# Eleven expert tiles in place of thirteen in a mixture-of-experts layer, with six blocks given out by the counts

## The reference, cut to what matters

```python
g_idx = top_1(softmax(hf @ w_rg + b_rg))          # group, 4 of them
e_idx = top_2(softmax(le[g_idx]))                 # 2 experts in the group
combine = weights of the 2 chosen experts, 0 for the other 14
a = einsum('bsd,edf->bsef', h, w_gate)
u = einsum('bsd,edf->bsef', h, w_up)
hid = silu(a) * u * combine
x = x + einsum('bsef,efd->bsd', hid, w_down)
```

## Time and profile before

| | |
|---|---|
| median of 3 runs | 499.16 us (497.79 to 499.41) |
| profiled execution | 500.98 us |
| its span, first to last instruction | 499.1 us |
| mean granted TensorE clock | 0.976 |
| expert part, first gate_up to the end | 323.1 to 499.1 us |
| PE busy | 466.0 us, 93% of the span |

### The profile page before, as it was taken

One profiled execution on the slowest core, in us unless ns is written; L12 is line 12 of the kernel. 1 busy time (PEld: TensorE's weight loads), 2 busy tenths in 40 slices (PEclk: granted clock), 3 DMA queues, 4 the chain that ended last, 5 costly groups with the idle time before them and its releaser, 6 DMA issues.

```text
span 499.1 us, 7640 instructions
## 1 busy us (share of the span) xinstructions
PE 466.0 (93%) x2826; PEld 227.5 (46%) x2826; DVE 214.7 (43%) x660; ACT 147.6 (30%) x340; POOL 152.8 (31%) x163
## 2 busy tenths in 40 slices
PE   5999999999999999999999999897999999998982
PEld 2545544445555565555556556633333333343320
DVE  2133644434764545355556757645122222231310
ACT  1321512326555555444342543400001011000000
POOL 1150788774499910000000211210351111111121
PEclk9999999999999999999999999778999999999997
DMA  8999960007000000193010459888499999999531
GB/s 308 396 412 367 404 266 1 1 0 270 5 1 1 1 2 0 49 412 131 0 44 2 145 195 378 309 314 325 153 358 384 391 374 403 388 375 400 183 57 26
DMA packets 28873, 102.66 MB, mean 206 GB/s; under 512 B 3744, under 2 KB 5280, under 8 KB 28448
## 3 DMA queue, kind: packets, MB, share of 16 engines
q1 hardware_dynamic: 22640, 88.25, 45.8%
q0 software_dynamic: 4176, 8.42, 7.0%
q10 hardware_dynamic: 2016, 5.46, 2.9%
HBM read 79.50 MB, written 29.44 MB: 218 GB/s over the span
## 4 chain that ended last, share of the span: by engine, by line
PE 77%; DMA 13%; DVE 4%; issue 2%; ACT 2%; POOL 1%; POOLq 0%; SPq 0%; DVEq 0%; ACTq 0%
PE bank L1344 21%; PE bank L1683 14%; PE bank L1514 10%; PE bank L1328 6%; PE bank L1707 6%; DMA arena<-in_w_gu 6%; PE bank L1416 5%; PE bank L1433 5%; PE bank L1379 3%; DMA arena<-slot_rows 3%; DMA slot_rows<-arena,small 3%; PE bank L1664 2%; PE bank L1457 2%; DMA arena<-in_w_in_lat 1%; DVE arena L1001 1%
## 5 line engine op out<-in xcount | busy, mean ns | idle before, releaser
L1344 PE MATMUL bank<-arena 128*128 128x512 f32 (+1 forms) x256 | 111.1, 584 | 5.7 <-DMA arena<-in_w_in_lat 5.7
L1683 PE MATMUL bank<-arena 128*32 128x512 f32 x832 | 96.3, 614 | 1.8 <-DMA arena<-in_w_gu 1.8
L1344 PEld LDWEIGHTS bank<-arena 128*128 128x128 f32 x256 | 48.2, 195 | 53.7 <-issue 53.2
L637 POOL DMA_INDIRECT out<-arena x13 | 20.2, 1550 | 134.3 <-DVE arena L1274 101.3
L1328 PEld LDWEIGHTS bank<-arena 128*128 128x128 f32 (+1 forms) x356 | 42.8, 140 | 35.7 <-issue 33.9
L1514 PE MATMUL bank<-arena 128*128 128x512 f32 x112 | 54.1, 605 | 0.6 <-issue 0.6
L1683 PEld LDWEIGHTS bank<-arena 128*32 128x32 f32 x832 | 26.8, 113 | 59.9 <-issue 57.5
L1328 PE MATMUL bank<-arena 128*128 128x128 f32 (+1 forms) x356 | 51.4, 277 | 2.7 <-ACT arena L711 1.9
L1707 PE MATMUL bank<-arena 128*32 128x512 f32 x416 | 47.1, 593 | 1.0 <-DVE arena L1267 1.0
L1001 DVE COPY arena<-bank 128x512 f32<-128x512 f32 (+2 forms) x64 | 35.7, 580 | 20.5 <-PE bank L1328 20.5
L873 ACT ACTIVATE arena<-bank 128x256 f32<-128x256 f32 x13 | 5.0, 383 | 129.7 <-PE bank L1683 129.7
(11 more groups left out here) (176 smaller groups left out, 502.4 us busy)
## 6 DMA issues: line engine op xcount, KB each, us to landing
arena<-in_w_gu SPq DMA_DIRECT2D x17, 2048.0 KB, 22.1
arena<-in_w_dn SPq DMA_DIRECT2D x17, 1024.0 KB, 22.7
slot_rows<-arena SPq DMA_DIRECT2D x1, 11822.0 KB, 48.3
arena<-slot_rows ACTq DMA_DIRECT2D x10, 514.0 KB, 7.3
arena<-in_w_out SPq DMA_DIRECT2D x2, 2048.0 KB, 8.1
arena<-in_x_turned SPq DMA_DIRECT2D x4, 512.0 KB, 8.1
arena<-in_x SPq DMA_DIRECT2D x4, 512.0 KB, 13.3
arena<-in_w_in_k SPq DMA_DIRECT2D x1, 2048.0 KB, 14.8
```

The lines of the kernel that those rows point to most:

```text
L1344: last = nc.tensor.matmul(product_bank(i)[:, 0:width], hT[:, t, k, :], w[:, k, :], start=(k == 0), stop=(k == KD - 1))
L1683: last = nc.tensor.matmul(GU[g % 2][BLK * b:BLK * (b + 1), :], xT[g % 2][:, k, BLK * b:BLK * (b + 1)], w_gu[n % RING][:, k, :], start=(k = ...
```

## The change

ITEMS becomes 11, and no extra tile runs unless the counts ask for it (up to 15 can, under conditions). The tiles are laid out by a table, in which FREE is a block whose place is found at run time:

```diff
-CAP, BLK = 96, 32
-ITEMS = E * CAP // P
+LAYOUT = [[0, 1, 2, 3], [0, 0, 1, 1], [2, 2, 3, 3], [4, 4, 5, 5], [FREE, 6, 6, 7], [FREE, 7, 8, 8], [FREE, 9, 9, 10],
+          [FREE, 10, 11, 11], [FREE, 12, 12, 13], [FREE, 13, 13, 14], [14, 14, 15, 15]]
+ITEMS = len(LAYOUT)
+LAST_USE = [1, 1, 2, 2, 4, 4, 5, 5, 6, 9, 8, 9, 9, 9, 9, 10]
+BUFFER = [0, 1, 2, 3, 4, 5, 0, 1, 2, 3, 4, 5, 0, 1, 2, 4]
+EXTRA = 15
-        LAST = ITEMS
+        LAST = ITEMS - 1
```

```diff
-            for g in range(LAST):
-                for n in range(RING, E + 1):
-                    if last_item(n - RING) == g - 1:
-                        sp.wait_ge(s_dn, 2 * g)
-                        load_dn(n, expert(n))
...
+            for g in range(ITEMS):
+                for n in range(RING, E):
+                    if LAST_USE[held_before(n)] == g:
+                        sp.wait_ge(s_gu, g + 1)
+                        load_gu(n, n)
+                for n in range(RING, E):
+                    if LAST_USE[held_before(n)] == g - 1:
+                        sp.wait_ge(s_dn, 2 * g)
+                        load_dn(n, n)
```

A token can have its two rows in one tile now, one in the free block and one in an own block. So a tile with a free block is added in two DMAs, 32 rows and then all 128 with the first 32 masked, and each add waits for the one before:

```diff
+            def add_rows(g, at, n):
+                nc.gpsimd.indirect_dma_start(
+                    out=out_rows, out_offset=bass.IndirectOffsetOnAxis(ap=at[0:n], axis=0),
+                    in_=y_sb[g % 2][0:n], in_offset=None,
+                    bounds_check=SEQ - 1, oob_is_err=False, compute_op=ALU.add).then_inc(s_add[g % 2], 16)
...
+                if loads_of(g)[0] == FREE:
+                    add_rows(g, tag_row[:, g, 0:1], BLK)
+                    pool.wait_ge(s_add[g % 2], added_before(g) + 16)
+                    add_rows(g, own_row[:, g - FREE_0, 0:1], P)
+                else:
+                    add_rows(g, tag_row[:, g, 0:1], P)
...
-            for g in range(ITEMS):
-                if g >= 2:
-                    added(g - 2)
+            for g in range(LAST):
+                if g > 0:
+                    added(g - 1)
                 add(g)
                 if g < 2:
                     overflow(2 * g)
                     overflow(2 * g + 1)
```

Rows for free blocks come with the overflow sends. So ACT loads no rows of tile 4 or a later one before all those sends have landed, and PE turns no tile in step 2 and two in step 3:

```diff
+            silu(0)
+            act.wait_ge(s_disp[1], 16 * TOP * 2)
+            load_x(3)
+            left_y(0)
+            silu(1)
+            silu(2)
+            left_y(1)
+            act.wait_ge(s_over, 16 * TOP * T)
+            for g in (4, 5, 6):
+                load_x(g)
+            for g in range(3, LAST + 1):
...
+        def turned_in(g):
+
+            return {2: (), 3: (4, 5)}.get(g, (g + 2,) if g + 2 <= LAST else ())
```

The matmuls of a free block take their weights from an address in a register, read twice a tile:

```diff
+                        if n == FREE:
+                            w = arena[:, bass.ds(free_at[g][0] + k * 2 * F, 2 * F)]
...
+            def free_places(g):
+
+                if g == FREE_0:
+                    pe.wait_ge(s_free, 1)
+                i = g - FREE_0
+                free_at[g] = [pe.value_load(v[0:1, i:i + 1], min_val=0, max_val=int(max(kbs) * KB))
+                              for v, kbs in ((gu_at, GU_KB), (dn_at, DN_KB))]
```

More of the change, by code:

```diff
@@ L58 @@
 K_FLOOR = K_LOW + E
-NK = K_FLOOR + E
+K_CAP = K_FLOOR + E
+K_FROM = K_CAP + E
+K_END = K_FROM + E
+K_MOST = K_END + E
+K_GU = K_MOST + E
+K_DN = K_GU + E
+K_LEAST = K_DN + E
+K_GONE = K_LEAST + FREES
+K_OWN = K_GONE + FREES
+NK = K_OWN + 1
+GU_KB = (16, 48, 120, 32, 64, 0)
+DN_KB = (80, 171, 195, 179, 187, 136)
 TILES = ITEMS + EXTRA
@@ L331, in loads_of, with buffer_of, nth_load, held_before @@
         def loads_of(g):
[L333 to L338, removed]
+            return LAYOUT[g] if g < ITEMS else [E + g - ITEMS] * 4
+        def buffer_of(n):
+            return BUFFER[n] if n < E else n % RING
+        def nth_load(n):
+            return sum(buffer_of(m) == buffer_of(n) for m in range(n + 1))
+        def held_before(n):
+            return max(m for m in range(n) if BUFFER[m] == BUFFER[n])
+        def own_loads(g):
+            return sorted(set(loads_of(g)) - {FREE})
+        def adds_of(g):
+            return 16 * (2 if loads_of(g)[0] == FREE else 1)
         def added_before(g):
-            return 16 * (g // 2)
+            return sum(adds_of(i) for i in range(g % 2, g, 2))
         def passes(eng, extra):
@@ L349, in passes @@
             with ExitStack() as more:
-                for i in range(1, EXTRA):
+                for i in range(EXTRA):
                     more.enter_context(eng.If(tiles > i))
@@ L1213, in extras_out @@
[L1213 to L1220, removed]
+                link(nc.vector.tensor_tensor(beyond, counts, table(K_CAP), ALU.subtract))
@@ new lines, in extras_out @@
+                link(nc.vector.tensor_scalar(wanted, beyond, 1.0, None, ALU.is_gt))
+                for bound in range(BLK, max(FREE_MOST) * BLK, BLK):
+                    link(nc.vector.scalar_tensor_tensor(wanted, beyond, bound + 1.0, wanted, ALU.is_gt, ALU.add))
+                link(nc.vector.tensor_tensor(wanted, wanted, table(K_MOST), ALU.min))
+                link(nc.vector.tensor_copy(sum_a, wanted))
+                running(sum_a, sum_b, ALU.add)
+                link(nc.vector.tensor_tensor(sum_a, sum_a, wanted, ALU.subtract))
@@ L1221, in extras_out @@
+                link(nc.vector.scalar_tensor_tensor(x_rows, f_blocks, -float(BLK), beyond, ALU.mult, ALU.add))
+                link(nc.vector.tensor_scalar(x_tmp, x_rows, 1.0, None, ALU.is_gt))
+                for bound in range(P, SEQ, P):
+                    link(nc.vector.scalar_tensor_tensor(x_tmp, x_rows, bound + 1.0, x_tmp, ALU.is_gt, ALU.add))
+                link(nc.vector.tensor_copy(x_start, x_tmp))
+                running(x_start, x_end, ALU.add)
                 link(nc.vector.tensor_copy(x_end, x_start))
@@ L1299, in _ @@
                 tile_tags(g)
+            places_out()
+            extra_places_out()
             for g in range(1, LAST + 1):
@@ L1780, with block_row, table @@
     p = np.arange(P, dtype=f32)
-    mine = (P * p[:ITEMS] + p[:, None]) // CAP
-    mine[:, 0] = p // BLK
-    for g in (1, 2):
-        mine[:, g] = 2 * (g - 1) + p // (2 * BLK)
+    mine = np.repeat(np.array(LAYOUT, f32).T, BLK, axis=0)
+    def block_row(n, i):
+        at = [P * g + BLK * b for g, row in enumerate(LAYOUT) for b, m in enumerate(row) if m == n]
+        return at[i]
+    def table(v):
+        return np.tile(np.array(v, f32), (P, 1))
+    least = [min(n for n in range(E) if FIRST_USE[n] <= g <= LAST_USE[n]) for g in FREE_TILES]
     konst = np.concatenate([
         np.triu(np.ones((P, P), f32), 1), np.ones((P, P), f32), np.tile(p[:E], (P, 1)),
-        np.tile(np.where(p[:E] < EARLY, P - BLK + 2 * BLK * p[:E], CAP * p[:E]), (P, 1)), np.tile(p[:EXTRA], (P, 1)), np.tile(p[:E] % G, (P, 1)), p[:, None] + P * p[:T] - FAR,
-        np.full((P, 1), FAR), mine, np.tile(np.where(p[:E] < EARLY, BLK - P - BLK * p[:E], 0), (P, 1)),
-        np.tile(np.where(p[:E] < EARLY, BLK, 0), (P, 1))], axis=1).astype(f32)
+        table([block_row(n, 1) - BLK for n in range(E)]), np.tile(p[:EXTRA], (P, 1)), np.tile(p[:E] % G, (P, 1)),
+        p[:, None] + P * p[:T] - FAR, np.full((P, 1), FAR), mine,
+        table([block_row(n, 0) - block_row(n, 1) + BLK for n in range(E)]),
+        np.tile(np.where(p[:E] < EARLY, BLK, 0), (P, 1)),
+        table([BLK * b - 0.5 for b in BLOCKS]), table(FREE_FROM), table([min(d, FREE_TILES[-1]) + 1 for d in LAST_USE]),
+        table(FREE_MOST), table([GU_KB[BUFFER[n]] * 256 for n in range(E)]),
+        table([DN_KB[BUFFER[n]] * 256 for n in range(E)]), table(least), table([float(g == GONE_AT) for g in FREE_TILES]),
+        np.where(p < BLK, 2 * FAR, FAR)[:, None]], axis=1).astype(f32)
     def by_expert(v, blocks):
```

182 lines of the change are left out of this document (118 added, 64 removed).

## The result

| | before | after |
|---|---|---|
| median | 498.48 us (4 runs, 497.73 to 499.41) | 509.8 us (4 runs, 509.05 to 510.76) |
| ratio to before | | 1.0224 (95%: 1.0191 to 1.0257) |
| span of the profiled execution | 499.1 us | 509.0 us |
| mean granted TensorE clock | 0.976 | 0.949 |
| matmuls in the expert part that gate and up take (L1683, L1819) | 832 | 704 |

The account below looks back on a forecast made before the run. PE was taken to bound the kernel, with weights close behind. 499.1 - 25.1 (tiles) + 18.2 (stall and clock) + 20.9 (chain of adds) = 513.1 us, forecast as 513 us, range 492 to 526.

Parts of the forecast that it names:

- The tiles: PE, expert part: two tiles of 11.68 us and a 1.76 us weight wait go, 25.1 us less.
- DVE: Counting before hidden(0): 29 more operations make it 1.6 us late, covered by other waits; cost 0, without cover 3.3 us.
- Registers: PE reading weight addresses into registers: hidden behind queued matmuls, cost 0, upper bound 12 us over six tiles.
- The stall: PE before tile 4 idles 14 us for overflow rows; with the lower clock, 18.2 us added.
- The pairs: Tiles 4 to 9: a 32-row then a 128-row add in series, 18.6 us loaded, 11.3 quiet; chain adds 20.9 us.
- Weights: Weight loads for PE: every gate_up finds its weights, cost 0; the stream alone would give about 485 us.
- the end: After the pairs end at 505.6 us, tile 10's add lands 6.0 us later and 1.5 us end the span: 513.1.
- (1): Adds at their quiet price all along: end at 496.9 us, or 492.2 if PE binds; chance 0.18.
- (2): Sends land before 378 or rows come at once, adds hidden: 474 us by PE, 485 by weights; chance 0.08.
- (3): Dearer adds, the 32-row add at a full one's price, pairs of 20.4 and 13.8 us: 525 us; chance 0.07.
- (4): Not eleven tiles, an extra tile runs through another routing: at least 15 us more, 528 us; chance 0.05.

Follow-up runs that it names:

- early sends: Changed kernel with all eight overflow sends right after the add of tile 0, not half behind the add of tile 1: 496.06 us, 0.9974 of before.
- a quarter of the weights: Changed kernel whose gate, up and down weight loads for places 10 to 15 move a quarter of their bytes: 495.51 us.
- both costs and the order of loads removed: Changed kernel with all overflow sends after tile 0's add, no 32-row adds, and down loads ahead of gate and up loads from step 5: 485.31 us.
- both edits: Changed kernel with all eight overflow sends right after the add of tile 0 and without the 32-row adds: 489.9 us.

## Why the prediction was right, point by point

**The tiles.** Two steps of PE went, and its cadence stayed 11.68 us. Right. PE's busy time fell by 19.3 us and not by 23.4, for some of the work ran at the lower clock level.

**DVE.** hidden(0) ran at 337.43 instead of 336.05, 1.4 us late (forecast 1.6). A thing that wasn't forecast came with it: PE idled 3.61 us and down(0) ran at the lower clock level, 6.39 us instead of 3.64 (granted clock 0.56 in 339.1 to 345.4). So gate_up(1) started 0.9 us later than before (347.57 against 346.66), although its rows were there. It ended at 354.6 us in both kernels all the same, because it took 7.07 us at the full clock and 8.01 before, part of it at the lower level. That the cost is 0 is partly luck.

**Registers.** Forecast 0, measured 0.4 us within the spread.

**The stall.** Forecast: sends landed at 384, the turn at 391.3, gate_up(4) from 395 to 404.5. Measured: the loads issued at 384.75, the turn at 391.68, gate_up(4) from 396.6 to 405.0. The second load landed 2.6 us after the first, not 1.6; the lower clock took 1.3 us of gate_up(4), not 2.5. The two errors are of opposite sign, and gate_up(5) started at 409.61, forecast 409.4. The experiment with early sends takes this wait away, and shows that it moves the whole chain of adds.

**The pairs.** First add at 421.6, measured 422.21. The add of tile 3 took 11.19 us, not 9.3, and landed at 421.40, 0.5 us after the results of tile 4 were ready; a longer one would have moved the whole chain, and the forecast had no term for it. The five pairs of tiles 4 to 8: 72.7 us forecast, 73.05 measured (422.21 to 495.26). That is nearer than the parts deserve: one by one 18.6, 17.8, 12.5, 12.5 and 11.3 us were forecast and 19.5, 16.3, 15.0, 10.5 and 11.7 measured. The 32-row add beside full queues took 6.70 and 5.63 us, not 7.5. The 128-row add in the same place took 11.25 and 9.14, not 9.3. In quiet the 32-row add took 3.2 to 3.6 us for 3.5, the 128-row add 5.4 to 6.6 for 6.0.

**Weights.** Forecast 0: every gate_up finds its weights. Every gate_up did, but down(6) waited 1.51 us. It isn't on the chain: the results of tile 6 are not added before 458.07.

**The term that was wrong: the end.** The sum had the add of tile 10 behind the landing of both adds of tile 9. The kernel before does wait there: behind its loop stand `added(LAST - 2)` and `added(LAST - 1)`, and then `add(LAST)`. The change takes both waits out, which the passage of the diff shown above leaves out. In the changed kernel the loop with `added(g - 1)` ends before LAST, and `add(LAST)` has no wait for it. The two adds went out 1.86 us apart. Making the kernel wait there costs 4.7 us in the median (514.46 against 509.8), and the span of that kernel is 513.2 us, where the sum had 513.1. The changed kernel's span is 509.0 us, so the missing wait is the size of the 4.1 us by which the span was missed, to within the spread of the runs. The other terms were off too, and their errors cancel.

**The rivals.** (1), adds at their quiet price, would have been 496.9 us: the kernel with a quarter of the weights comes near it by hand and runs at 495.5, but its pairs of tiles 4 and 6 are still at 14.2 and 12.4 us, and it lacks the wait at the end that the 496.9 contain, so that the two numbers agree in part by chance. (2), no stall and hidden adds, 485 us by the weights: 485.3 with both costs and the order of loads removed. (3) and (4) did not come.
The Trainium skill (DMA: Bandwidth & Descriptors, section Anatomy of one DMA, SWDGE path) gives 2.0 us and the bytes at 436 GB/s for a DMA that GpSimd issues, by which an estimate is 2.3 us for 32 rows and 2.9 for 96. The adds took 3.2 to 3.6 and 5.4 to 6.6 us in quiet, up to 6.7 and 11.25 beside the weight loads, counted from the issue. The measurement decides.

**The gain that was there.** PE's last matmul ends where it did before (489.6 and 489.9 us), so PE lost its 25 us on the way. Some 18 us went at tiles 4 and 5 (gate_up(5) starts at 409.61, before at 391.05): 14.4 us of waiting for rows, the rest for the second load and at the lower clock. 1.5 us went to down weights, and some 4.5 to down(9), which waited 2.77 us behind the adds and then took 5.34 us for 3.62. The loss itself is the tail in which only adds run: 19.4 us behind the last matmul, 9.3 before.

## What to carry to other kernels

An engine at 93% is not the only thing to read before cutting its work: price every serial chain per step (here landing of one add to issue of the next), beside the traffic that is there, and compare it with the new step time; 9.3 us hid under 11.68, two adds did not. A wait that was harmless at the last tile (for all overflow rows) is a stall when it moves to tile 4; so issue what it waits for earlier, too. And read the end of a loop in the diff as closely as its middle: one missing wait was the largest error of the sum.

## What the runs showed of the hardware

- From issue to landing an indirect accumulating DMA takes as long when it names 128 rows of which 32 are masked (5.38 us at tile 7, 6.06 at tile 8, early sends) as when it names 96 (5.41 and 5.96 us), with the weight loads over. With 32 rows it is 3.2 to 3.6 us (changed kernel).
- Beside the weight loads (DMA share 1.00 in 430 to 460 us) the same DMAs take 5.6 to 6.7 us (32 rows) and 9.1 to 11.25 us (128 rows). With a quarter of the weight bytes (share 0.47) they came at 3.2 to 4.65 and 6.0 to 7.95 us.
- PE worked at the lower clock level not only after the 14.4 us wait but after idle stretches of 3.61 us (down(0) 6.39 us for 3.64, granted clock 0.56), 6.26 us (down(6) with both edits, 6.07 us for 3.62, 0.59) and 2.77 us (down(9), 5.34 us for 3.62, 0.67). After the 1.51 us before down(6) of the changed kernel the clock was 1.00 (3.64 us).
